# Value projections for four heads at once, tokens stationary, rows passed through DRAM

## The reference, cut to what matters

```python
gate, (na_q, na_k, na_v, na_z, f_u, f_z, d_q, d_k, d_v, d_z, g) = mixer_input(x, cvec, norm_g, w_mod, b_mod, w_in)
...
o = einsum('bhrqiw,bhriwd->bhrqd', p_loc, vg) + einsum('bhrqn,bhnd->bhrqd', p_ctx, v_ctx)   # na
a = (p[:, :, 0] - lam * p[:, :, 1])
return einsum('bhqk,bhkd->bhqd', a, v)                                                       # df
...
y = y + sigmoid(gate) * ((outs[b] * silu(zs[b])) @ w_branch_l[b])
```

## Time and profile before

| | |
|---|---|
| median of 3 runs | 2861.0 us (2860.9 to 2862.08) |
| profiled execution, its own time | 2863.71 us |
| its span, first to last instruction | 2861.9 us |
| PE busy | 2807.7 us, 98% of the span |
| DVE, ACT, POOL busy | 1336.5, 1099.8, 610.3 us |
| share of PE on the chain that ended last | 94% |
| matmuls with a projection unit's shape (L758) | 7920 in 330 units |
| transposes of values (L783) | 144 |
| mean granted clock | 0.995 |

### The profile page before, as it was taken

The page is one execution under the profiler, slowest core; times in us unless marked ns, Lnnn a source line. Parts: engine busy times, 40 slices in busy tenths (PEclk is TensorE's granted clock), DMA queues, the critical chain, the costliest instruction groups (busy, mean ns, idle before and its releaser), DMA issues.

```text
span 2861.9 us, 43764 instructions
## 1 busy us (share of the span) xinstructions
PE 2807.7 (98%) x18148; PEld 2698.4 (94%) x18148; DVE 1336.5 (47%) x2325; ACT 1099.8 (38%) x2043; POOL 610.3 (21%) x312
## 2 busy tenths in 40 slices
PE   6999999999999999999999999999999999999998
PEld 4999999999999999999999999999999999999997
DVE  4243454224646555446343445423355656553643
ACT  4443444223444444412344444432234444443232
POOL 0221211222121221122431221113221121211241
PEclk9999999999999999999999999999999999999999
DMA  5332323111111112254421221220211111215532
GB/s 210 110 120 76 108 90 127 59 57 56 40 49 49 57 35 100 91 201 137 132 85 68 68 78 39 75 77 27 82 44 42 48 65 41 89 56 186 168 107 94
DMA packets 83701, 246.55 MB, mean 86 GB/s; under 512 B 9136, under 2 KB 30128, under 8 KB 82480
## 3 DMA queue, kind: packets, MB, share of 16 engines
q1 hardware_dynamic: 83504, 243.76, 25.0%
HBM read 189.72 MB, written 54.00 MB: 85 GB/s over the span
## 4 chain that ended last, share of the span: by engine, by line
PE 94%; DVE 2%; DMA 1%; ACT 1%; issue 1%; SPq 1%; DVEq 0%; POOL 0%; POOLq 0%; ACTq 0%
PE ps L758 49%; PE ps L741 18%; PE ps L861 7%; PE ps L797 5%; PE ps L1093 4%; PE ps L948 2%; PE ps L1084 2%; PE ps L929 2%; PE ps L1013 1%; DMA wmod<-w_mod 1%; PE ps L817 1%; PE ps L775 1%; PE ps L806 1%; PE ps L783 1%; PE ps L1051 1%
## 5 line engine op out<-in xcount | busy, mean ns | idle before, releaser
L758 PE MATMUL ps<-hhi,whi 128*128 128x384 f32 x2640 | 917.9, 348 | 5.7 <-DVE obuf L1968 3.3
L758 PE MATMUL ps<-hhi,wlo 128*128 128x384 f32 x2640 | 886.4, 336 | 0.0
L758 PE MATMUL ps<-hlo,whi 128*128 128x384 f32 x2640 | 884.3, 335 | 0.0
L2070 POOL TENSOR_TENSOR wlo<-wraw,whi 128x1024 fp32r<-128x1024 f32 (+1 forms) x188 | 411.9, 2191 | 1979.4 <-ACT whi L1179 1979.4
L758 PEld LDWEIGHTS ps<-hhi,whi 128*128 128x128 f32 x2640 | 500.0, 189 | 37.3 <-issue 23.3
L758 PEld LDWEIGHTS ps<-hlo,whi 128*128 128x128 f32 x2640 | 497.1, 188 | 0.9
L758 PEld LDWEIGHTS ps<-hhi,wlo 128*128 128x128 f32 x2640 | 496.1, 188 | 0.0
L1179 ACT ACTIVATE whi<-wraw 128x1024 fp32r<-128x1024 f32 (+1 forms) x188 | 174.5, 928 | 232.0 <-PE ps L741 212.5
L1779 DVE TENSOR_TENSOR ptl<-ps,pth 128x512 fp32r<-128x512 f32 (+1 forms) x144 | 82.1, 612 | 275.6 <-ACT pth L1364 275.3
L1527 ACT ACTIVATE aTh<-ps 128x512 fp32r<-128x512 f32 (+1 forms) x200 | 96.4, 482 | 259.5 <-PE ps L1084 259.5
L1518 ACT ACTIVATE e<-ps,stat 128x1152 f32<-128x1152 f32 x144 | 162.0, 1125 | 55.1 <-DVE stat L1936 55.1
(11 more groups left out here) (221 smaller groups left out, 4726.7 us busy)
## 6 DMA issues: line engine op xcount, KB each, us to landing
wraw<-w_in SPq DMA_DIRECT2D x128, 512.0 KB, 4.3
gates_dram<-gst SPq DMA_DIRECT2D x48, 576.0 KB, 3.1
gth<-gates_dram SPq DMA_DIRECT2D x48, 576.0 KB, 4.7
mraw<-w_mod SPq DMA_DIRECT2D x32, 512.0 KB, 3.8
wraw<-w_branch SPq DMA_DIRECT2D x48, 256.0 KB, 2.7
bias<-rpb SPq DMA_DIRECT2D x8, 1280.0 KB, 6.6
outs_dram<-obuf SPq DMA_DIRECT2D x16, 576.0 KB, 3.1
oraw<-outs_dram SPq DMA_DIRECT2D x16, 576.0 KB, 3.7
```

Source lines behind the costliest of these rows:

```text
L758: x = mm(ps[:, bank, 0:CH], a[:, s % 2, k, :], b[:, k, n * CH:(n + 1) * CH], start=(k == 0 and a is whi and b is hhi), stop=(k == KT - 1 a ...
L2070: g_.tensor_tensor(lo[:, 0:kt, :], wraw[:, n % 2, 0:kt, :], hi[:, 0:kt, :].bitcast(F32), ALU.subtract).then_inc(S.w_lo, 1)
```

## The change

The v chunks leave the fillers and the df preamble. At the first neighbourhood head of each layer, the weights of four value chunks at a time (na, then df) are split into `rows_hi` and `rows_lo`, and `value_rows` multiplies with a token tile of `hhi`/`hlo` stationary and the four heads' weights moving: 24 matmuls of 512 columns give 128 tokens x 4 heads x 128 channels in one PSUM bank. There are nine token tiles for na and nine for df. ACT copies each to `vstage`, SP stores it to the new tensor `rows_dram` (and tile 8 to the output), and the rows of one head are read back into `vrow` with its cached values; ACT makes the whole high part (`value_high`) and POOL the whole low part (`value_low`) in one instruction each. The transposes, `vT` and DVE's `value_low` go. `rows_hi`/`rows_lo` of df lie where `mraw`, the second bias buffer and the probabilities lie, so that loads into these start after the rows. Every neighbourhood step now has one unit; three gate chunks per layer move from na to df, where they take the places of the v chunks.

```diff
-    kinds = {"na": ("qkgvg", "qkgvg", "qkgv", "gggg"), "df": ("qgkgvg", "qgkgvg", "qgkgvg", "gggggg")}[ph][p]
-    at = {"na": (0, 2, 4, 5), "df": (9, 12, 15, 18)}[ph][p]
+    kinds = {"na": ("qkg", "qkg", "qkg", "ggg"), "df": ("qgkggg", "qgkggg", "qgkggg", "gggggg")}[ph][p]
+    at = {"na": (0, 1, 2, 3), "df": (6, 10, 14, 18)}[ph][p]
...
+                if ph == "na" and p == 0:
+                    out += [("v", l, of, h) for of in ("na", "df") for h in range(HEADS)]
...
             # SP
+            def rows_out(l, ph):
+                job = 2 * l + (ph == "df")
+                for t in range(TILES):
+                    i = TILES * job + t
+                    src = vstage[:, i % 2, :].rearrange("p (h n) -> p h n", n=P)
+                    sp.wait_ge(S.v_copied, i + 1)
+                    sp.dma_start(rows_dram[job, :, t].rearrange("h p n -> p h n"), src).then_inc(v_store[i % 2], 16)
+                    if t == LT:
+                        out = {"na": new_na_v, "df": new_diff_v}[ph]
+                        sp.dma_start(out[l].rearrange("h p n -> p h n"), src).then_inc(v_store[i % 2], 16)
+                    if ph == "na":
+                        weights_to(CHUNK["v", l, "df", 0] + min(t, 3) + 3)
...
+            def value_rows_in(l, ph, p, n):
+                job = 2 * l + (ph == "df")
+                if p == 0:
+                    for i in range(2):
+                        sp.wait_ge(*stored_rows(TILES * (2 * l + 2), i))
                 if p:
                     sp.wait_ge(S.vc_lo, n)
-                sp.dma_start(vraw[:], cv[l, p]).then_inc(S.vc_load, 16)
+                sp.dma_start(vrow[:, 0:TILES, :], rows_dram[job, p].rearrange("t p n -> p t n")).then_inc(S.vc_load, 16)
+                sp.dma_start(vrow[:, TILES, :], (cache_na_v if ph == "na" else cache_diff_v)[l, p]).then_inc(S.vc_load, 16)
...
                 cached(l, "na", 0, 2 * HEADS * l)
+                for r in "qk":
+                    keep_streaming((r, l, "na", 0))
+                weights_to(CHUNK["v", l, "df", 1] + 1)
+                rows_out(l, "na")
+                sp.wait_ge(S.w_used, SPLIT_NO["v", l, "na", HEADS - 1] + 1)
                 sp.dma_start(bias[:, 0], rpb[l, 0]).then_inc(S.bias_load, 16)
-                for r in "qkv":
-                    keep_streaming((r, l, "na", 0))
+                rows_out(l, "df")
+                value_rows_in(l, "na", 0, 2 * HEADS * l)
                 for p in range(HEADS):
...
+                    else:
+                        sp.wait_ge(S.w_used, SPLIT_NO["v", l, "df", HEADS - 1] + 1)
+                        if l + 1 < DEPTH:
+                            mod_to(2)
                     if p + 1 < HEADS:
                         cached(l, "na", p + 1, n + 1)
...
             # PE
+            def value_rows(l, ph, t0, t1):
+                for t in range(t0, t1):
+                    i = TILES * (2 * l + (ph == "df")) + t
+                    if t == 0:
+                        pe.wait_ge(S.w_lo, SPLIT_NO["v", l, ph, HEADS - 1] + 1)
+                    if i >= 2:
+                        pe.wait_ge(S.v_copied, i - 1)
+                    out = ps[:, 6 + i % 2, :].rearrange("p (h n) -> p h n", n=P)
+                    for k in range(KT):
+                        for a, b in ((hhi, rows_hi), (hlo, rows_hi), (hhi, rows_lo)):
+                            x = mm(out, a[:, k, t * P:(t + 1) * P], b[ph][:, :, k, :], ...)
...
-                    values_to_rows(n, v, 0, 5)
                     unit(z, 0)
-                    pe.wait_ge(S.na_o, NA_OUTS * u)
-                    values_to_rows(n, v, 1, 4)
                     unit(z, 1)
...
+                    else:
+                        unit(z, 2)
+                        value_rows(l, "na", 0, TILES)
+                        value_rows(l, "df", 0, TILES - 2)
+                        pe.wait_ge(S.x_split, 2 * n + 2)
+                        scores(0)
+                        value_rows(l, "df", TILES - 2, TILES)
+                        pe.wait_ge(S.v_copied, 2 * TILES * (l + 1))
...
-                for r in "qkv":
-                    if r in "qk":
-                        pe.wait_ge(*evacuated("w", l, "fn", HEADS - 2 + "qk".index(r)))
+                for j, r in enumerate("qk"):
+                    pe.wait_ge(*evacuated("w", l, "fn", HEADS - 2 + j))
                     for i in range(NC):
                         unit((r, l, "df", 0), i)
...
             # ACT, first head
+                        split_to(SPLIT_NO["v", l, "na", 2] + 1)
+                        evacuate(z, 1)
+                        split_to(SPLIT_NO["v", l, "na", 3] + 1)
+                        evacuate(z, 2)
+                        for t in range(TILES):
+                            rows_copied(l, "na", t)
+                            split_to(SPLIT_NO["v", l, "df", min(t, HEADS - 1)] + 1)
...
                     for t, units in enumerate(na_steps(l, p)):
+                        if p == 0 and t == 1:
+                            value_high(n, "na")
```

More of the change, by code:

```diff
@@ L77, in in_units @@
 def in_units(c):
[L79 removed]
+    return c[0] in "qkg" or (c[0] == "z" and c[2] != "fn")
 STREAM = plan()
@@ L85 @@
 SPLIT_NO = {c: i for i, c in enumerate(SPLIT)}
-JOBS = [c for c in SPLIT if not in_units(c) and c[0] != "o"]
+JOBS = [c for c in SPLIT if not in_units(c) and c[0] not in "ov"]
 JOB_NO = {c: i for i, c in enumerate(JOBS)}
@@ L106, in gate_no @@
     return c[1] * 3 * KT + c[3]
-NA_TWO = {15: (0, 1, 2, 3, 4, 5), 12: (0, 1, 2)}
 NA_OUTS = LT // 2 + 1
 def na_steps(l, p):
[L115 to L123, removed]
+    return [[(c, n)] for c in fillers(l, "na", p) for n in range(NC)]
+GATES_NA = 6
 DF_TWO = (0, 1, 2, 3, 4, 5, 6, 7)
@@ L164, in unit_banks @@
         for ph in ("na", "df"):
-            order = [((r, l, ph, 0), n, 3 * i + n if i < 2 else (6, 7, 0)[n]) for i, r in enumerate("qkv") for n in range(NC)]
+            order = [((r, l, ph, 0), n, 3 * i + n) for i, r in enumerate("qk") for n in range(NC)]
             for p in range(HEADS):
@@ L289, in build @@
     kraw = pl("kraw", [P, TK])
-    vT = pl("vT", [P, T])
+    vrow_at = pl.at
+    vrow = pl("vrow", [P, TILES + 1, P])
     high_at = pl.at
@@ L490, in slot_free, with stored_rows, rows_done @@
             return SPLIT_NO["o", c[1] - 1, "", "qk".index(c[0])] + 1
-        return s - 1
+        if c[0] == "v":
+            return SPLIT_NO["q", c[1], "na", 0] + 1
+        if SPLIT[s - 1][0] == "v":
+            return SPLIT_NO["k", c[1], "na", 0] + 1
+        if SPLIT[s - 2][0] == "v":
+            return SPLIT_NO["z", c[1], "na", 0] + 1
+        return s - 1
+    def stored_rows(i, half):
+        return v_store[half], 16 * sum(2 if j % TILES == LT else 1 for j in range(half, i, 2))
+    def rows_done(i):
+        job, t = divmod(i, TILES)
+        if t == TILES - 1:
+            return S.w_used, SPLIT_NO["v", job // 2, ("na", "df")[job % 2], HEADS - 1] + 1
+        return S.v_rows, (TILES - 1) * job + t + 1
     def pair_no(l, ph, p):
@@ L719, in _ @@
                 result(NC - 1, half)
-            sp.wait_ge(S.k_store, 32 * 2 * HEADS * DEPTH)
+            sp.wait_ge(S.k_store, 16 * 2 * HEADS * DEPTH)
+            for i in range(2):
+                sp.wait_ge(*stored_rows(TILES * 2 * DEPTH, i))
             sp.wait_ge(S.y_store, 16 * 2 * NC)
@@ L778, in first_units @@
                                     x.then_inc(unit_done(c, n)[0], 1)
[L780 to L790, removed]
+            def value_rows(l, ph, t0, t1):
[8 more added lines that the diff above has]
+                        for a, b in ((hhi, rows_hi), (hlo, rows_hi), (hhi, rows_lo)):
+                            x = mm(out, a[:, k, t * P:(t + 1) * P], b[ph][:, :, k, :],
+                                   start=(k == 0 and a is hhi and b is rows_hi), stop=(k == KT - 1 and b is rows_lo))
+                    x.then_inc(rows_done(i)[0], HEADS if t == LT else 1)
             def score(outs, t, k0, k1):
@@ L1223, in raw_free @@
                     act.wait_ge(S.x_split, 2 * pair_no(l, ph, p))
[L1224 to L1227, removed]
+                if n == NC - 1 and kind == "k":
+                    act.wait_ge(S.k_store, 16 * pair_no(l, ph, p))
             def query_high():
@@ L1342, in _ @@
                 key_high(2 * HEADS * l)
-                for i in range(NC):
-                    evacuate(("v", l, "na", 0), i)
                 for p in range(HEADS):
@@ L1499, in _ @@
                 query_high()
-                for i in range(NC):
-                    evacuate(("v", l, "df", 0), i)
                 act.wait_ge(S.rope_done, 2 * l * HEADS + 2)
@@ L2110, in _ @@
                     n, cs = n0 + p, fillers(l, "na", p)
-                    split_to(SPLIT_NO[cs[0]] + 1)
-                    cached_low(n, "na")
+                    split_to(SPLIT_NO[cs[0]] + (2 if p == 0 else 1))
+                    value_low(n, "na")
                     split_to(SPLIT_NO[cs[-1]] + 2)
```

178 lines of the change are left out of this document (82 added, 96 removed).

## The result

The changed kernel takes 2897.9 us (median of 4 runs, 2894.0 to 2898.3) against 2861.4 before on the same chip: slower, by a ratio of 1.0123 (95% interval 1.011 to 1.0135), or 36.6 us. The prediction, 2888, was 10 us low; the time lies in its range.

A forecast was written before the change was run, and what follows sets the result against it. The prediction took PE, busy 98% of the span, as the bound: 46 us of new idle and slow matmuls, less 19 us gained, made it 27 us slower, 2888 us for the runs, range 2858 to 2904.

The forecast's parts named there:

- transposes gone: PE at 16 heads: removing the value transposes saves 1.0 us per head, 16 us (14 to 18.5).
- wide matmuls (at the price of long runs): PE's row tiles: 512 columns at 228.7 ns, extrapolated from 256 and 384, save fixed cost, 3 us taken.
- weights ahead of the rows: Before the row tiles: PE waits for value chunks to be loaded and split, 5 us (0 to 9).
- `mraw`, all heads, less 0.8 before: Layer 0, heads 0 to 3: modulation loads arrive late on SP's queue and PE waits, 19.6 us.
- rotation, both layers: First df head: fewer units cover DVE's passes on k and POOL's `kl`; PE waits 12 us (4 to 14).
- clock: Behind four new PE waits over 4 us: matmuls run slower, 1.86 us each, 7 us (0 to 13).
- gate units at df heads: Df heads: gate chunks take the places of v chunks, at no cost.
- in proportion, no gain: Bound for PE's row tiles: 512 columns cost in proportion to 384, 231.2 ns, so nothing is gained.
- loads land as if alone: Rival on SP's loads: they land in 3.8 us, third modulation load and heads 1 and 2 free; 2874 us, chance 0.13.
- covered: Rival for the whole kernel: every new wait of PE is hidden, giving 2842 us; chance 0.11.
- rotation free: Rival at the first df head: DVE's passes meet no POOL work, 2 us per layer; 2876 us, chance 0.09.
- wide matmuls cheap: Rival on PE's row tiles: 512 columns take 213 ns, 13 us less, 2875 us; chance 0.09.

The follow-up runs named there:

- -13 (runs): Kernel before the change with each of its 144 value transposes on PE done twice: 2875.1 us, 13.4 more.
- the last run above: Changed kernel with loads, splits and rotation work reordered, plus adjacent weight columns, an earlier second value chunk and a later wait for the last row copy: 2856.1 us.
- the first run: Changed kernel with each `mraw` load put ahead of the loads before it on SP's queue: 2879.7 us, 18 less.

## Why the prediction was right, and where it was short

Its steps one by one, in us over the kernel before:

| step | predicted | shown |
|---|---|---|
| transposes gone | -16 | -13 (runs) to -16 (pieces) |
| wide matmuls (at the price of long runs) | -3 | +2 |
| weights ahead of the rows | 5 | 2.8 |
| last copy | 2 | 1.4 |
| `mraw`, all heads, less 0.8 before | 19.6 | 17.9 |
| first `value_low`, layer 1 | 0.5 | 0 |
| rotation, both layers | 12 | 12.6 |
| clock | 7 | 15 |
| gate units at df heads | 0 | 2.3 |
| PE's other waits | 0 | -1.6 |

With 16 for the transposes the right column sums to 36 us, with 13 to 39; 36.6 were measured. The same sum for the last run above, whose waits of PE are 8.0 us longer together than before and which loses no more to the clock, gives -16 + 2 + 8 = -6; 5 less were measured. So the mechanisms were the right ones and the signs too. Two terms were mis-sized and one was missing, by 15 us together; that the forecast was only 10 low is in part luck, as the smaller terms erred by 6 the other way.

*The clock.* The prediction charged 1.86 us for each of four waits over 4 us. Six stretches ran at a low clock, since waits of 3.4 and 3.2 us (heads 1 and 2) had one behind them as well, and they cost 15 us by their windows, 1.5 to 3.2 each; filling the waits gave back 13.3 of it. The row that priced it, 72 matmuls behind a 2.4 us wait, lies at the low end of that.

*The wide matmuls.* The line through 256 and 384 columns gave 228.7 ns; it is 233.5, so 864 of them take 201.7 us where 1152 of the old ones took 199.8. Even "in proportion, no gain" (231.2) was too good: a loss had not been bounded. The Trainium skill (TensorE: Matmul & The Clock Gate, Back-to-back issue gap) has N/2.4 + 2.5 ns for an isolated gap, an estimated 215.8 at 512 columns and 162.5 at 384; the measured 233.5 and 176.1 agree with neither.

*A term was missing*: with gate chunks in the places of v chunks at the df heads, PE waits six times some 0.4 us for ACT's copy of a gate unit. The prediction counted that exchange as even; no run tells what in it makes the wait.

The rest held. Single-unit steps showed no wait for DVE or ACT. SP's queue order is the cause of the `mraw` waits (the first run), and "loads land as if alone" fell with the third load's 8.01 us. The rivals "covered", "rotation free" and "wide matmuls cheap" fell by the waits, the 3.54 and 3.24 us passes, and 233.5 ns.

## What to carry to other kernels

Work taken off a saturated engine pays only if every operand still comes before the engine asks: here 16 us of transposes were bought with 37 us of late operands and 15 us of slow clock behind them, and a reordering of SP's queue and of POOL's work around one rotation (with a few smaller edits) turned a loss of 1.2% into a gain of 0.2% (0.1 to 0.3). Count what stands ahead of each load on an in-order queue when a load is added, and look at what the units that you move were hiding. Charge each new wait of PE of a few microseconds with 1.5 to 3 us more for the clock behind it.

## What the runs showed of the hardware

- What a wait costs in clock does not grow with its length: behind 6.9 us of waiting 9.2 us ran at 0.78 of the clock, behind 3.2 us 8.1 us ran at 0.61; behind 1.1 us (head 3) the modulation took 0.64 where it takes 1.08 behind the longer waits. Needless matmuls in the waits kept the clock at 1.0 in five stretches of six and made the program 13 us faster; behind the 1.8 us that stayed open the clock fell.
- A tensor-tensor pass of 128 x 1024 on DVE takes 1.23 us with POOL at rest and 2.97 to 3.54 when it begins under a POOL subtraction, and then it ends 1.1 us behind that, as if it ran after it and not beside it. A subtraction that begins under a DVE pass goes from 2.40 to 3.36 likewise. The Trainium skill (Trainium Architecture — The Big Picture, What this means for kernel authors) says that DVE and GpSimd contend for a shared port pair by an exclusive lock; the passes agree with it.
- With a weight load for each matmul, matmuls start 118.1, 173.4 and 233.5 ns apart at 256, 384 and 512 columns, each in a form of its own. In the form of the row tiles they start 176.1 apart at 384 and 233.5 at 512, so the last 128 columns cost 57.4, about a quarter of the whole: a wider one buys next to no fixed cost back. Four pieces of 128 columns cost what 512 adjacent ones do.
